# The first pair of experts of a layer gathered in three parts, the second expert's tokens behind the first expert's gate products

## The reference, cut to what matters

```
cap = EC_CAPACITY * s // N_EXPERTS                       # 2 * 512 // 16 = 64
aff = softmax(h @ w_router)
gates, idx = top_k(swapaxes(aff, 1, 2), cap)
xe = h[b_idx, idx]                                       # 64 tokens of 1024 features for each expert
hid = silu(einsum('becd,edf->becf', xe, w_gate)) * einsum('becd,edf->becf', xe, w_up)
ye = einsum('becf,efd->becd', hid, w_down) * gates[..., None]
return zeros_like(h).at[b_idx, idx].add(ye)
```

## Time and profile before

| | us |
|---|---|
| median of 3 runs | 2036.38 (2033.71 to 2037.26) |
| the profiled execution, its own time | 2033.39 |
| its span | 2031.5 |
| PE busy | 1828.1 (90%) |
| DVE busy | 798.8 (39%) |
| ACT busy | 519.8 (26%) |
| L1673, the expert products | 685.4 in 3072 records |
| DMA over the span | 459.98 MB, mean 226 GB/s |

### The profile page before, as it was taken

One profiled execution on the slowest core, in us unless ns is written; L12 is line 12 of the kernel. 1 busy time (PEld: TensorE's weight loads), 2 busy tenths in 40 slices (PEclk: granted clock), 3 DMA queues, 4 the chain that ended last, 5 costly groups with the idle time before them and its releaser, 6 DMA issues.

```text
span 2031.5 us, 44863 instructions
## 1 busy us (share of the span) xinstructions
PE 1828.1 (90%) x19992; PEld 954.7 (47%) x19992; DVE 798.8 (39%) x1448; ACT 519.8 (26%) x1025; POOL 239.9 (12%) x294
## 2 busy tenths in 40 slices
PE   7899999988996959999899988899895999999987
PEld 4466666666666433333333336666443433333332
DVE  7755765666563241111221123666614112221211
ACT  3344445344343211110001012555511110001010
POOL 2203203303302110000000001111111000000000
PEclk9999999999999979999999999999997999999999
DMA  4101101101112759999999971100064899999997
GB/s 122 35 4 38 44 10 36 44 20 32 38 48 80 281 228 396 427 427 427 427 428 427 427 310 59 68 23 18 5 270 187 365 426 427 427 427 428 427 427 315
DMA packets 85001, 459.98 MB, mean 226 GB/s; under 512 B 16709, under 2 KB 49866, under 8 KB 60234
## 3 DMA queue, kind: packets, MB, share of 16 engines
q1 hardware_dynamic: 82794, 449.78, 54.5%
q0 software_dynamic: 2016, 7.34, 0.9%
HBM read 449.23 MB, written 7.86 MB: 225 GB/s over the span
## 4 chain that ended last, share of the span: by engine, by line
PE 57%; DMA 20%; issue 8%; DVE 7%; ACT 3%; DVEq 2%; POOL 1%; POOLq 1%; SPq 0%; ACTq 0%; PEldq 0%; another core or an unknown queue 0%
DMA arena<-in_moe_w_down 17%; PE banks L1673 17%; PE banks L544 9%; PE banks L1378 5%; PE banks L872 5%; PE banks L1719 4%; DMA arena<-in_moe_w_up 2%; ACT arena L2204 2%; PE banks L2189 2%; PE banks L830 1%; PE banks L2165 1%; PE banks L1638 1%; PE banks L821 1%; PE banks L561 1%; DMA arena<-in_positions 1%
## 5 line engine op out<-in xcount | busy, mean ns | idle before, releaser
L1673 PE MATMUL banks<-arena 128*64 128x512 f32 x3072 | 685.4, 600 | 51.1 <-DMA arena<-in_moe_w_down 33.5
L1673 PEld LDWEIGHTS banks<-arena 128*64 128x64 f32 x3072 | 223.1, 138 | 477.1 <-issue 434.9
L1778 DVE TENSOR_TENSOR arena<-arena,banks 128x512 f32<-128x512 f32 x128 | 88.0, 687 | 329.0 <-PE banks L1719 329.0
L544 PE MATMUL banks<-arena 128*128 128x512 f32 x384 | 187.1, 613 | 1.8 <-ACT arena L584 1.8
L872 PE MATMUL banks<-arena 64*64 64x64 f32 x7168 | 145.8, 222 | 34.2 <-issue 26.9
L872 PEld LDWEIGHTS banks<-arena 64*64 64x64 f32 x7168 | 133.1, 136 | 77.6 <-issue 59.0
L1224 POOL TENSOR_TENSOR arena<-arena 128x512 f32<-128x512 f32 x80 | 102.5, 1308 | 431.7 <-DVE arena L1281 431.7
L1732 ACT ACTIVATE arena<-banks 128x512 f32<-128x512 f32 x32 | 19.1, 597 | 411.7 <-PE banks L1673 411.7
L1719 PE MATMUL banks<-arena 128*128 128x512 f32 x256 | 113.7, 597 | 3.0 <-ACTq L1741 3.0
L1767 DVE SCALAR_TENSOR_TENSOR arena<-arena,banks 128x512 f32<-128x512 f32 x32 | 33.6, 1051 | 206.6 <-PE banks L1673 206.6
L1378 PE MATMUL banks<-arena 128*128 128x512 f32 x256 | 112.6, 594 | 1.8 <-POOLq L399 1.3
(11 more groups left out here) (299 smaller groups left out, 2199.7 us busy)
## 6 DMA issues: line engine op xcount, KB each, us to landing
arena<-in_moe_w_gate SPq DMA_DIRECT2D x64, 2048.0 KB, 36.0
arena<-in_moe_w_up SPq DMA_DIRECT2D x64, 2048.0 KB, 38.3
arena<-in_moe_w_down SPq DMA_DIRECT2D x60, 2048.0 KB, 38.5
out_dram<-arena SPq DMA_DIRECT2D x12, 512.0 KB, 2.6
arena<-in_x SPq DMA_DIRECT2D x8, 512.0 KB, 5.9
arena<-in_rw_wr SPq DMA_DIRECT2D x8, 512.0 KB, 4.1
arena<-in_rw_wk SPq DMA_DIRECT2D x8, 512.0 KB, 5.8
arena<-in_rw_wv SPq DMA_DIRECT2D x8, 512.0 KB, 6.1
```

The lines of the kernel that those rows point to most:

```text
L544: last = nc.tensor.matmul(b[:, :], w_sl[:, n, k, :], xmix[n][:, k, :], start=(k == 0), stop=(k == ND - 1))
L1673: last = nc.tensor.matmul(b[z * CAP:(z + 1) * CAP, :], st[:, k, :], ring[g % RING][:, k, z * 512:(z + 1) * 512], start=(c % 2 == 0 and k = ...
L1778: nc.vector.tensor_tensor(xs, xs, b[:, :], ALU.add).then_inc(free[COMB[j]], 1)
```

## The change: the order of PE's first products

The first gather now makes only the first expert's tokens: still 32 matmuls with a 128x128 stationary operand, but with 64 moving columns in place of 128, and the feature halves one after the other (all token tiles of the first half, then all of the second) in place of alternating. ACT copies each half, now 64 columns a block. The first gate chunk waits only for the copy of the first half, the second chunk for that of the second.

Behind the two gate chunks of the first expert stands a second gather, `gather_second_pe`: again 32 matmuls with the same 128x128 stationary operands, with the 64 moving columns of the second expert, into one bank (bank 6). The four transposes of `combination_pe` stand behind it. One ACT copy, behind the first `Tanh`, brings the bank into `xeT`; PE waits for it before the second expert's gate. POOL's row fetch for pair 1 waits for the second gather. Both layers have this once. Pairs 1 to 7 are as before.

```diff
+            order += [] if i else [(("x", 0, "second"), 6)]
@@ gather_first_pe
-            bs = [open_job(pe, xj, ("x", 0, z)) for z in range(2)]
+            for z in range(2):
+                b = open_job(pe, xj, ("x", 0, z))
+                for t in range(NT):
+                    for k in range(4):
+                        last = nc.tensor.matmul(b[:, k * CAP:(k + 1) * CAP], h_tok[:, t, (4 * z + k) * P:(4 * z + k + 1) * P], pick[:, t, 0:CAP],
+                                                start=(t == 0 and k == 0), stop=(t == NT - 1), skip_group_check=True)
+                last.then_inc(full[z], 1)
+
+        def gather_second_pe(pe, layer):
+            xj = xjs[layer]
+            b = open_job(pe, xj, ("x", 0, "second"))
             for t in range(NT):
-                for z in range(2):
-                    for k in range(4):
-                        last = nc.tensor.matmul(bs[z][:, k * P:(k + 1) * P], h_tok[:, t, (4 * z + k) * P:(4 * z + k + 1) * P], pick[:, t, :],
-                                                start=(t == 0 and k == 0), stop=(t == NT - 1), skip_group_check=True)
-                    if t == NT - 1:
-                        last.then_inc(full[z], 1)
+                for k in range(ND):
+                    last = nc.tensor.matmul(b[:, k * CAP:(k + 1) * CAP], h_tok[:, t, k * P:(k + 1) * P], pick[:, t, CAP:2 * CAP],
+                                            start=(t == 0 and k == 0), stop=(t == NT - 1), skip_group_check=True)
+            last.then_inc(full[6], 1)
             combination_pe(pe, 0, xj)
@@ moe_pe
                 def up_to_hidden(name, e, c):
                     for h in range(2):
+                        if i == 0 and c == 0:
+                            job_read(pe, xj, ("x", 0, h))
                         chunk_into(name, c + h, xeT[:, 4 * h:4 * h + 4, e * CAP:(e + 1) * CAP])
...
-                for z in range(2):
-                    job_read(pe, xj, ("x", i, z))
+                if i:
+                    for z in range(2):
+                        job_read(pe, xj, ("x", i, z))
                 up_to_hidden(("gate", i, 0), 0, 0)
+                if i == 0:
+                    gather_second_pe(pe, layer)
                 up_to_hidden(("up", i, 0), 0, 2)
+                if i == 0:
+                    job_read(pe, xj, ("x", 0, "second"))
                 up_to_hidden(("gate", i, 1), 1, 4)
@@ moe_act
+                    if i:
+                        nc.scalar.copy(xeT[:, 4 * z:4 * z + 4, :].rearrange("p k s -> p (k s)"), b[:, :]).then_inc(free[z], 1)
+                    else:
+                        nc.scalar.copy(xeT[:, 4 * z:4 * z + 4, 0:CAP], b[:, 0:4 * CAP].rearrange("p (k s) -> p k s", k=4)).then_inc(free[z], 1)
...
                     nc.scalar.activation(th, b[:, :], ACT.Tanh, scale=0.5).then_inc(tanh_ready, 1)
+                    if i == 0 and e == 0:
+                        b = job_full(act, xj, ("x", 0, "second"))
+                        nc.scalar.copy(xeT[:, :, CAP:2 * CAP], b[:, :].rearrange("p (k s) -> p k s", k=ND)).then_inc(free[6], 1)
@@ moe_pool
-                job_full(pool, xj, ("x", i - 1, 1))
+                job_full(pool, xj, ("x", i - 1, 1) if i > 1 else ("x", 0, "second"))
```

More of the change, by code:

```diff
@@ L1726, in moe_act @@
                     b = job_full(act, xj, ("x", i, z))
-                    nc.scalar.copy(xeT[:, 4 * z:4 * z + 4, :].rearrange("p k s -> p (k s)"), b[:, :]).then_inc(free[z], 1)
+                    if i:
+                        nc.scalar.copy(xeT[:, 4 * z:4 * z + 4, :].rearrange("p k s -> p (k s)"), b[:, :]).then_inc(free[z], 1)
+                    else:
+                        nc.scalar.copy(xeT[:, 4 * z:4 * z + 4, 0:CAP], b[:, 0:4 * CAP].rearrange("p (k s) -> p k s", k=4)).then_inc(free[z], 1)
                 for e in range(2):
```

## The result

| | us |
|---|---|
| before, median | 2035.63 (2033.71 to 2037.26, 4 runs) |
| changed, median | 2054.06 (2050.59 to 2058.09, 4 runs) |
| ratio | 1.0092, 95% interval 1.0069 to 1.0114 |
| predicted | 2041.9 (2034 to 2047) |

The changed kernel is 18.4 us slower. The side was forecast, the size was not: +5.5 was predicted, and the time lies above the range and above each rival. The executions of a kernel lie within 0.6% of one another, but for one of e8's 12, which took 3546.69 us and which its ratio leaves out.

What follows compares the result with a forecast made beforehand. Bound: the weight-chunk transfers, so bytes moved when the stream becomes full. Missing bytes cost 2.5 us in layer 0 and 3.1 in layer 1, together +5.5: 2041.9 us for the median, range 2034 to 2047.

Steps and rivals of the forecast that it cites:

- 111.6 ns at either clock: Both gathers: each 64-column record costs its 128-column load, 111.6 ns at low or full clock, so 7.14 us a gather.
- The upper end of 213: Gather records at the low clock: 213 ns each, named as the upper end of the range.
- The 98 ns: Low end of a gather record's cost, from 16-column records: both gathers 0.87 us shorter, +5.5 becomes +2.0.
- The clock's rise: First gather: the granted clock was 0.50 to 754.8 us, then 1.00; rival 2 let it rise later.
- rival 2: Gathers: no relief at the low clock, first gather 9.28 and 8.70 us as before; +9.2, 2045.6 us; chance 0.15.
- the 15.90 us of idling: Ahead of the first gather: the clock was low since PE had stood idle for 15.90 us.
- First gather and chunk 0: Layer start: gather 7.14 us, no transposes or copy wait ahead; chunk 0 starts 3.02 and 2.45 us earlier.
- The second gather, the hole, the full stream behind it: Between chunks 1 and 2: 7.14 + 0.60 us, transfers idle some four us, then 427 GB/s to the layer's end.
- Chunk 12's delay: SP's issue of chunk 12, behind the second gather: 4.7 us later in layer 0, 5.3 in layer 1.
- The hidden parts: ACT's copies, DVE's combination copy and POOL's row fetch for pair 1: nothing on the path.
- Rival 1: Gathers: a record costs by its columns, 107 ns at low clock, 56 at full; -5.0, 2031.4 us; chance 0.12.
- rival 3: Transfer stream: the gap is made up, no change within 0.2%, about 2037 us; chance 0.15.

Runs made afterwards that it cites:

- e8: Kernel before plus 15 wide matmuls ahead of the gather, feature halves in order, combination transposes behind chunk 3, no second gather: 2029.72 us, ratio 0.9979.
- e9: Changed kernel plus 16 wide matmuls ahead of the wait for the slots and one behind the slots' transposes, keeping PE busy: 2034.11 us, ratio 1.0003.
- e1: Small program in place of the kernel: stretches of matmul records of several widths after idling; 64 records of 64 columns take 13.92 us at the low clock.
- e10: e9 with the second gather and the transposes moved behind chunk 3: 2033.71 us, ratio 1.0001 to the kernel before.
- e11: e8 with PE kept at work as in e9, so one 128-column gather at full clock: 2025.52 us, ratio 0.9962 to the kernel before.
- e7: e5 with the second gather and the transposes moved from behind chunk 1 to behind chunk 3: 2042.19 us, ratio 1.0047 to the kernel before.
- e12: e11 without any of the extra matmuls, so the kernel before with only the new order: 2031.62 us, ratio 0.9995.
- e5: Changed kernel plus 15 wide matmuls on PE while DVE chooses the tokens: 2050.14 us, ratio 1.0085 to the kernel before.
- e4: Changed kernel plus 28 wide matmuls on PE while DVE chooses the tokens, which made the gather start late: 2052.01 us, ratio 1.0096.

## Why the prediction was wrong

- **"111.6 ns at either clock"** is the step that failed. It held at the full clock (second gather 7.20 us, e9's first 7.29, predicted 7.14) and not at the low one: 216 ns. I bounded the low clock by one row, 4 records with 16 rows and 16 columns, 120 ns, and read it as a load of 128 columns. Those loads have 16 rows, and they are transposes; e1's matmuls with 128 rows and 16 moving columns take 216. Which of the two makes the four records fast no run shows. The nearest row was near in columns and in the clock, but not in rows or kind, and I let it outweigh the plain doubling from 111.6 to 213 in the gather itself. The upper end of 213 that I named was the right pace.
- **The 98 ns** at the lower end of the range was a misreading: of the six records' starts in that row the first two are 31 ns apart, the other four times 111 to 112. No matmul record with a 128x128 load went faster than the gather's 112.
- **The clock's rise** was the second step: it was taken over from the kernel before without being a step of the sum. I named it in rival 2 as an alternative to the slow records ("or the clock rises later"), when both come together: this narrow gather was slow at the low clock and didn't raise it. Rival 2 priced only the slow records up to the old moment of the rise, +9.2. What it left out: the 43 records behind that moment at 216 in place of 112, 4.5 us, and the first two chunks, 9.18 us in layer 0 for e9's 7.01. The reason that I gave for the low clock, the 15.90 us of idling, was off too: the clock shows 0.50 already from 731.0 to 731.8, in an idle time of 3.32 us ahead of the one named, and stays at 0.50 until the gather raises it.
- **First gather and chunk 0**: predicted 3.0 us earlier, measured 3.7 later after the gather's start (13.84 against 10.16).
- **The second gather, the hole, the full stream behind it**: right, in place and kind. Chunk 12's delay at full clock was forecast as 4.7 and 5.3, and e9 has 5.0 and 5.6. What follows from it was too dear: I left 2.2 us of slack, it is 3.3, so +5.5 should have been +3.4. The stream of the kernel before runs at 358 GB/s even from 769 to 773, so pausing there loses less than a full stream would: by that, 0.6 of the 1.1 us (4 us at 69 GB/s less, an estimate).
- **The hidden parts** (ACT's copies, DVE, POOL): right. The copies of the halves took 0.37 and no product waited for them. DVE's place was right only for the change itself (see e10).
- **Rival 1** (faster, cost by columns) is refuted by e11 against e9, **rival 3** by the result. That the side was right is in part luck: the path that I had priced, e9's, is 3.7 us by the layers and 0.4 by the medians, and most of the measured loss came by the step that I had wrong.
- The parts: e9 has the second gather's 1.7 and 2.0 us, and the changed kernel 8.6 and 8.3 more. Layer 0's 8.6 answer to 6.55 in the gather (13.84 - 7.29) and 2.2 in the first two chunks.

Open: e9, e10 and e11 are timed 1 to 4 us faster than the stretches of their layers alone add up to (e9: +3.7 by the layers, +0.4 by the medians; e10: +1.3 and 0.0; e11: -4.5 and -8.2), and e7 nearly 7 (+15.5 and +8.8). The single traces differ by more than that ahead of the first gather, where the work is the same, so I don't ascribe it. The extra matmuls didn't slow DVE's choice of the tokens beside them: e9's transposes of the slots start 16.91 us after the transposes ahead of the wait (734.69 to 751.60), before it was 16.92.

## What to carry to other kernels

Halving the moving columns of a matmul pays only while the stream is longer than the load. In float32 with 128x128 loads it wasn't here: 16 to 128 columns went at one pace, 112 ns at the full clock and 213 at the low one, and the split, which repeats the loads, doubled the time (7.29 + 7.20 for 7.34 us). Behind an idle time look at the clock first: here a group of narrow matmuls ran at half pace and did not raise the clock either, and keeping PE at work through the wait ahead of it was worth more (e11 against e12: 6.1 us, 0.3%) than the order of the gather, whose own worth these runs can't tell from nothing. Where a saturated stream sets the end, price a delay by what it does to the next transfer's issue less its slack. Putting the extra work two chunks later helped by 1.2 us a layer (e10 against e9), but it moved the hole and did not fill it; and when an instruction moves, look at what the other engines do ahead of the work that frees a bank.

## What the runs showed of the hardware that I had not expected

- A float32 record with a 128x128 load took 213 ns from start to start at 1.2 GHz and 112 at 2.4, with 16, 64 and 128 moving columns alike at both; with a load of 64 columns 108 and 58 (e1).
- 64-column records with 128x128 loads did not raise the clock in 27.5 us from 0.50, but kept it at 1.00 for 28.7 us in e1. 16-column ones lost it. 96-column ones raised it after 4.3 us, and 64-column ones with loads of half the width after 3.3.
- Two idle times of 1.20 and 1.15 us, with 0.42 us of small transposes between them, stood ahead of e5's gather in layer 0, and its clock was down by the start; with 0.30 and no idle time (e9) it stayed up. e4, with only the second of them, stayed up too. But the length of the idle time alone does not settle it: e8's layer 1, behind 1.90 and 1.15 us, ran its whole 128-column gather at 1.00, and e7's layer 1, behind 1.83 and 1.15, began its 64-column gather at 1.00 and lost the clock 1.9 us into it. What decides these cases no run shows.
